# Delta scan: six pairs' state products for y, split around the two halves of T's products

## What is computed

```python
def step(S, inp):
    r_t, w_t, k_t, v_t, a_t, b_t = inp
    sa = jnp.einsum('bhij,bhj->bhi', S, a_t)
    S = S * w_t[:, :, None, :] + sa[..., None] * b_t[:, :, None, :] + v_t[..., None] * k_t[:, :, None, :]
    return S, jnp.einsum('bhij,bhj->bhi', S, r_t)
```

## Time and profile before

| | |
|---|---|
| median of 3 runs | 3695.01 us (3693.85 to 3695.46) |
| the profiled execution, its own time | 3697.57 us |
| its span, first to last instruction | 3695.7 us |
| TensorE products busy | 3485.9 us (94%) |
| TensorE weight loads busy | 3273.8 us (89%) |
| VectorE busy | 1539.7 us (42%) |
| ScalarE busy | 1129.0 us (31%) |
| GpSimd busy | 610.3 us (17%) |
| mean granted TensorE clock | 0.971 |

### The profile page before, as it was taken

How to read it: one execution, slowest core, us unless ns; L and a number is a source line. 1 busy time by engine, 2 the same in 40 slices (tenths; PEclk the granted TensorE clock), 3 DMA queues, 4 the chain that set the end, 5 groups by cost and what they waited for, 6 DMA issues and landing times. The chain is left out here.

```text
span 3695.7 us, 60384 instructions
## 1 busy us (share of the span) xinstructions
PE 3485.9 (94%) x25902; PEld 3273.8 (89%) x25902; DVE 1539.7 (42%) x2513; ACT 1129.0 (31%) x2105; POOL 610.3 (17%) x717
## 2 busy tenths in 40 slices
PE   8899979999999999998899995987999999999998
PEld 8898769989999999995698884866998999999997
DVE  6335464344332332335226666555334332232233
ACT  6223263223220221225435521544223321121123
POOL 1100112002110110121312375422100110010012
PEclk9999989999999999998899997998999999999999
DMA  6422311202111111115646676953200111111111
GB/s 227 109 60 64 108 28 48 79 18 47 46 46 46 46 46 46 46 35 155 227 142 216 212 202 149 248 137 88 86 29 24 46 46 50 45 49 47 46 41 65
DMA packets 457384, 323.08 MB, mean 87 GB/s; under 512 B 105134, under 2 KB 435214, under 8 KB 453870
## 3 DMA queue, kind: packets, MB, share of 16 engines
q1 hardware_dynamic: 402874, 280.72, 26.3%
q10 hardware_dynamic: 43876, 18.99, 2.0%
q0 software_dynamic: 10368, 19.51, 1.6%
HBM read 232.29 MB, written 86.96 MB: 86 GB/s over the span
## 5 line engine op out<-in xcount | busy, mean ns | idle before, releaser
L83 PE MATMUL ps<-am_y,am_wh 128*128 128x352 f32 x4944 | 1182.1, 322 | 12.4 <-PEq L2576 12.4
L83 PE MATMUL ps<-am_h,am_wh 128*128 128x352 f32 x3648 | 884.2, 324 | 1.2 <-DVE am_h L1415 1.2
L83 PEld LDWEIGHTS ps<-am_y,am_wh 128*128 128x128 f32 x4944 | 855.6, 188 | 14.7 <-issue 13.4
L83 PE MATMUL ps<-am_y,am_wl 128*128 128x352 f32 x2472 | 792.2, 320 | 0.0
L83 PEld LDWEIGHTS ps<-am_h,am_wh 128*128 128x128 f32 x3648 | 636.6, 188 | 4.2 <-DVE am_h L1415 1.4
L83 PE MATMUL ps<-am_h,am_wl 128*128 128x352 f32 x1824 | 588.6, 323 | 0.0
L83 PEld LDWEIGHTS ps<-am_y,am_wl 128*128 128x128 f32 x2472 | 463.9, 188 | 0.0
L83 PEld LDWEIGHTS ps<-am_h,am_wl 128*128 128x128 f32 x1824 | 342.7, 188 | 0.0
L1503 POOL TENSOR_TENSOR am_silu<-am_silu,rs 128x352 f32<-128x352 f32 x132 | 126.5, 960 | 1229.6 <-ACT am_silu L1359 1229.6
L1085 DVE TENSOR_TENSOR x<-ps,x 128x352 f32<-128x352 f32 x240 | 125.9, 525 | 461.8 <-PE ps L83 456.6
L83 PE MATMUL ps<-rw_parts,rw_wh 128*128 128x352 f32 (+1 forms) x1152 | 289.1, 333 | 18.9 <-PEq L2558 13.0
(11 more groups left out here) (328 smaller groups left out, 4628.3 us busy)
## 6 DMA issues: line engine op xcount, KB each, us to landing
am_w<-in_ffn_w SPq DMA_DIRECT2D x120, 512.0 KB, 3.8
rw_ra_d<-tb_rk SPq DMA_DIRECT2D x8, 1056.0 KB, 8.2
rw_kbt_d<-tb_gk SPq DMA_DIRECT2D x8, 1056.0 KB, 4.0
rw_gg_d<-tb_gk SPq DMA_DIRECT2D x8, 1056.0 KB, 6.5
fr_w<-in_xa_wk SPq DMA_DIRECT2D x8, 1024.0 KB, 5.5
fr_w<-in_xa_wv SPq DMA_DIRECT2D x8, 1024.0 KB, 5.3
am_w<-in_xa_wq SPq DMA_DIRECT2D x16, 512.0 KB, 3.8
am_w<-in_xa_wo SPq DMA_DIRECT2D x16, 512.0 KB, 3.8
```

What stands on the lines that cost most here:

```text
L83: mm = nc.tensor.matmul(out, l, part, start=start and n == 0, stop=stop and n == 2)
```

## The change

Of the six pairs' state products for y that stood behind both halves of T, pairs 2, 3 and 4 now stand behind T's first half and pairs 5, 6 and 7 behind its second. The call moves into the loop over q:

```diff
@@ -575,7 +575,7 @@
                                               tt[r, l % SLOTS, sub, p // 2].rearrange("r h t -> r (h t)"),
                                               z[r, p // 2, :], start=True, stop=True)
                     mm.then_inc(u_done, 1)
-                y_part(n, lambda p: S[:, p, :], lambda p: ra[:, s, p, 1], True, range(2, PAIRS))
+                    y_part(n, lambda p: S[:, p, :], lambda p: ra[:, s, p, 1], True, range(2 + 3 * q, 5 + 3 * q))
                 for q in range(2):
                     pe.wait_ge(u_out, 2 * n + q + 1)
                     for p in range(4 * q, 4 * q + 4):
```

## The result

The launch got longer, by less than forecast. Over 12 launches the changed kernel has a median of 3704.38 us (3696.97 to 3710.78), the kernel before, in 12 launches beside it, 3697.11 us (3693.72 to 3704.91). The ratio is 1.0016, 95% interval 1.0009 to 1.0024: 5.9 us, between 3 and 9 (the two medians lie 7.3 us apart, the means of the launches 6.2). The forecast was 3703.9 us and 8.9 us more; the interval lies across the bound of 0.2%, so that the kernel is slower is clear of the noise, and that it is slower by over 0.2% isn't.

The account below looks back on a forecast made before the run. The prediction took TensorE's serial chain in the scan's 4.50 us step as the bound. Switches cost 8.7 + 1.2 = 9.9 us, less 1.0 for late instructions: 3695.0 + 8.9 = 3703.9 us, range 3699.5 to 3707.

Parts of the forecast that it names:

- The path: Scan step of 4.50 us: TensorE's work between T and the state products counts in full, VectorE's additions of u lie beside it.
- (a): Splitting T in the scan step adds two switches of product shape on TensorE: 0.29 us per step, 0.40 at the lower clock.
- rival B: Switches at T are free or hidden, T's second half only 0.17 us late: launch the same, 3695.0 us; chance 0.10.
- The products moved at 0.058 us each: Three y pairs moved between T's halves delay its second half by three slots of 0.058 us, 0.17 us.
- (b): T's second half ends about 0.46 us later, so the second addition of u waits; slack about 0.15 us, cost nothing.
- (d): Seven waits for late TensorE instructions in the scan each shrink by up to 0.29 us: at most 2.0 back, 1.0 taken.
- The sum: Over the scan's 33 steps: 30 x 0.29 + 3 x 0.40 = 9.9 us, less 1.0 = 8.9 us on the launch.
- Rival C: Switch price is paid in the scan, but late instructions and clock give part back: 4.9 us more, 3699.9; chance 0.14.
- A: The forecast itself: two more switches on the scan's path, 7.9 to 9.9 us more, 3702.9 to 3704.9; chance 0.60.
- The signs of being wrong: Step stays 4.50 us, exceeds 4.85 with a pause inside the state products, or scan stalls or clock change over 2 us.
- E: Second half's state products wait for u: 0.05 to 0.1 us per step more, 3705.6 to 3707.2 us; chance 0.12.

Follow-up runs that it names:

- the two of the last section: Against the kernel before, y pairs moved behind the state products, state double-buffered: pairs 2 to 7, ratio 0.9994; or four pairs ahead of T, four behind, ratio 0.9993.
- two and four pairs: Against the changed kernel, two y pairs behind T's first half and four behind its second, not three and three: step 4.79 us, median 3701.54 us, ratio 1.0008.
- four switches: Against the kernel before, y groups of two pairs behind T's first half, in the middle of its second and behind it: step 5.08 us, ratio 1.0023.
- The two pairs of profiles: Kernel before and changed kernel, each profiled twice without further edits: 32 intervals took 160.8 and 163.7 us before, 164.1 and 164.6 us changed.

## Why the prediction was right, and where it was not

- **The path** (TensorE's chain from T to the state products is serial, VectorE's additions lie beside it): right. In the six kernels in which y stands ahead of the state products every undisturbed step is what its TensorE groups add up to. In the two of the last section TensorE waited for VectorE as well.
- **Two switches at 0.29 us** (a): right. 0.29 with two and four pairs, 0.58 for four switches. The Trainium skill, page "TensorEngine Tiling (Array Packing)", section "Key Properties", says that changing the tiling mode drains TensorE; the trace agrees. Behind each of the four changes of shape in the step of the earlier trace rows the first weight load starts 0.067 or 0.068 us after the last one ahead of it has ended, where two groups of one shape overlap by 0.086 or 0.087 us. So rival B, that weight loads are pulled ahead across the switch, is out.
- **The products moved at 0.058 us each** (a): wrong, and the step was 0.40 in place of 0.29 for it. The pitch was read from groups of eight and six, which are even, and divided by their number. What those rows can't show is that the slot belongs to two pairs together; the diff, with three and three, is the first to have odd groups. The same page and section of the Trainium skill ("TensorEngine Tiling (Array Packing)", "Key Properties") say that different tiles can load and multiply in parallel; the equal length of three and four pairs agrees. This was the mis-sized term: 0.11 x 33 = 3.6 us too little.
- **The second addition of u** (b): right that it loses its place behind the first and is covered. It was forecast 0.91 us behind the first and stands 0.90 behind it (2448.74 - 2447.84).
- **Late instructions** (d): right in direction, wrong in size. I allowed one step's 0.29 for each of seven waits, 2.0 us at most, and took 1.0. The two pairs of profiles give 9 and 12 us back, waits and the clock behind them together. The waits went from 8.6 to 3.7 us in the first pair and from 11.2 to 3.2 in the second. What the 2.0 left out is that a slower step gives every block more time, so that some waits vanish and the clock falls less often behind them.
- **The sum**: 9.9 - 1.0 = 8.9 was near because two errors had opposite signs: 13.0 less some 7 is 5.9, where the 7 is only what the launches leave over. That the number came out near is luck. Rival C, price paid and given back in part by instructions and clock, which I gave 0.14, describes the mechanism better than A does, and its 4.9 us lie nearer to 5.9 than A's 8.9. The range was right for it; "slower by over 0.2%", which I gave 0.68, is not shown: the ratio is 1.0016.
- **The signs of being wrong**: one was met, and one in half. The scan's stalls changed by more than 2 us, by 4.9 and 8.0, so by the prediction's own terms step (d) failed. The step exceeds 4.85, but without the pause inside the state products that E needs.

That the loads cause the lateness is shown by leaving them out, and that blocks of 256 instructions come late by the traces. Open is why the next packet starts later under the loads, and how much of the time given back is waits and how much is clock.

## What to carry to other kernels

Read the price of a switch of product shape on TensorE from the start-to-start distances of neighbouring groups before splitting one; a moved product pays only if it fills an idle stretch, and here there was none. Where products run two to a slot, keep groups even. And a chain of short instructions under heavy loads can lose time to its own instruction supply, so a step made faster or slower by some amount doesn't move the launch by that amount: leave the loads out once to see the full price, and lay TensorE's waits for "issue" beside the packets of the instruction queue.

## What the runs showed of the hardware

- A switch between products of 64 by 128, 128 by 64 and 64 by 64 costs TensorE 0.145 us at 2.4 GHz (4.50, 4.79 and 5.08 us a step with none, two and four added).
- Three y pairs take 0.375 us between two switches, four take 0.381.
- With DMA engines 87% busy in the scan, 32 steps took 17 to 20 us more than undisturbed ones of 4.50 us, and 7 to 8 more than undisturbed ones of 4.90; without the loads from the fifth on 6 to 7 more in either, all in the first five steps.
- TensorE's instructions arrive in packets of 16,384 bytes, one for 256 recorded instructions. All 63 waits for "issue" of 0.3 us or more in 14 profiles of the scan end 1.3 to 1.7 us behind the end of one. The packet itself takes 1.1 to 1.2 us in the mean with and without the loads; its start comes in the mean 2.1 us behind the start of the block before under the loads, 0.5 without.
